# Mixers' branch gates and branch outputs computed token-major

## The chip, the cores and the metric

The kernel runs on one core of a Trainium2 chip. The metric is the device time of one execution in microseconds (us), shown as the median of several. TensorE is called PE here, VectorE DVE, ScalarE ACT, GpSimd POOL, and SyncE SP; SP issues the loads of the weights.

## The reference

Four blocks work on x, 256 tokens of 1024 features, in float32. Two of them (the layers) hold a feed-forward part, a mixer, and another feed-forward part; two more have other mixers and are not touched. A layer's mixer makes three branches of 512 features each from the normed h, gates them and projects the sum:

```
h      = rms_norm(x, mix_norm)
gl     = h @ w_in[:, last 3*1024]                  # three gates of 1024 features
y[0]   = mla_branch(...);  y[1] = gdn_branch(...);  y[2] = moba_branch(...)    # 256 x 512 each
merged = sum over n of  sigmoid(gl[n]) * (y[n] @ w_branch[n])                    # 256 x 1024
x      = x + merged @ w_out
```

The kernel takes tanh(gl / 2) and uses (tanh + 1) as the gate; the factor one half is applied where x is updated.

## The kernel before

**Units.** All weights come as one stream of units, 128 partitions of 1024 float32 numbers (512 KB). SP loads unit u into one of three raw buffers (`raw`, `load`, L492) as soon as the low half of unit u-3 is made. ACT rounds it to `w_hi` (`split`, L550, 128 x 1024), DVE makes `w_lo` = raw - `w_hi` (`split`, L1211). There are six slots; `split(u)` waits until unit u-6 is used (`unit_used`), and its place in the queues of ACT and DVE is written out by hand: `split(u + AHEAD)` with AHEAD = 5 stands where unit u is due on PE. Activations have halves too, `a_hi` and `a_lo`. A product takes three matmuls: high by high, high by low, low by high.

**Gates.** `gate_unit(l, i)` (L2342) makes 128 gate features of all 256 tokens with `fm` (L2196): for each of 8 pieces of K three matmuls with the weights stationary and 256 tokens moving, into the first half of bank 6 or 7 by turns. `gate_tile` (L679) on ACT takes the tanh of the bank, 128 x 256. There are 24 such units a layer. They are spread over the mixer to fill the time in which PE would wait for other engines: units 0 to 3 in the doubling steps that invert a triangular matrix (L2501 to L2528), 4 to 8 behind them, 9 to 17 in the first attention loop (`FILLS`, `LAST_FILL`, L211), 18 to 21 around the second attention's head, the rest in its loop.

**Branches.** `branch_unit(l, i)` (L2349), 12 a layer, makes 256 features of one branch output (two groups of 128, K = 4 x 128), 24 matmuls with 256 tokens moving, into bank 6 or 7 by turns. `merge` (L1446) on DVE multiplies the 512 columns with tanh + 1 and, from the second branch on, adds them to `msum`. Units 0 to 7 fill the second attention loop, units 8 to 11 follow it. ACT and DVE then make the high and low half of `msum`, which is feature-major (`mix_high` L907, and L1812), for the output product `km_tokens` (L2260), where the activations are stationary and 512 columns of the weights move: 12 matmuls a unit, 8 units, banks 0 to 3.

**Attention loop.** Each of its four steps has on PE: a fill, the next scores, the turn of the probabilities, a fill, probabilities by values. DVE takes the maxima (L1421 to L1429), ACT the exponentials (L691, L693), DVE normalises (L1437 to L1439), ACT copies the turned ones (L699). Ahead of the second loop PE turns queries and keys (L2604), which waits for the copies of the query product by ACT (L870 to L876) and for DVE (L1789 to L1797). POOL computes powers (L1131) and masks for the doubling steps (L1146).

Every engine works its own queue in order; a wait at its head holds all that follows.

## Time and profile before

| | |
|---|---|
| median of 3 runs | 1955.2 us (1954.77 to 1956.87) |
| profiled execution | 1960.22 us, span 1958.4 us |
| busy: PE, its weight loads, DVE, ACT, POOL | 99%, 89%, 75%, 56%, 5% |
| DMA from HBM | 327.91 MB, 168 GB/s over the span |
| first mixer, second mixer | from 197 to 497 us, from 869 to 1169 us |

A row of a timeline has the start and the length in us, the engine, the line of the kernel, the operation, what it writes and reads with sizes, and the count of instructions that were merged in it; idle time of the engine before it stands in brackets with what ended it. Matmuls overlap, so the pace of a stream is read from the starts, not from the lengths. All matmuls with an operand that was rounded to halves carry one line, L2155.

### The profile page before, as it was taken

Reading aid. Unit: us, or ns where it says so; the run is one execution under the profiler, and the core shown is the slowest. Engines: PE = TensorE matmul, PEld = TensorE weight load, DVE = VectorE, ACT = ScalarE, POOL = GpSimd, SP = SyncE. Lnnn points to the kernel's source line nnn. Section 1 sums busy time; section 2 is a strip of 40 time slices with the busy share of each in tenths; the row PEclk is TensorE's granted clock in tenths of the full one; section 3 lists DMA queues with packets and bytes.
Section 4 is the critical chain, followed back from the end, with each engine's and each line's share of the span. In section 5 each row is a group of like instructions: output and inputs, shape, how many; then the busy total and the mean of one; then the engine's idle time right before and its main releaser. Section 6 shows DMA issues by size and latency. Waiting matters only on the chain.

```text
span 1958.4 us, 35076 instructions
## 1 busy us (share of the span) xinstructions
PE 1930.7 (99%) x13137; PEld 1734.8 (89%) x13137; DVE 1469.8 (75%) x2252; ACT 1087.9 (56%) x1702; POOL 89.3 (5%) x61
## 2 busy tenths in 40 slices
PE   9999999999999999999999999999999999989999
PEld 8888899999888888889899998889898889879998
DVE  6777777667777777778667777777578888877887
ACT  6555764665555555556536644555345555765554
POOL 0000002010000000000120102000000000100000
PEclk9999999999999999999999999999999999999999
DMA  6656443344555655555424455655655665444554
GB/s 231 194 190 197 160 157 101 114 154 144 168 188 190 193 173 192 193 183 178 132 80 142 140 166 165 199 188 190 203 179 163 195 190 179 158 126 141 193 191 140
DMA packets 95798, 331.03 MB, mean 169 GB/s; under 512 B 10960, under 2 KB 16720, under 8 KB 95568
## 3 DMA queue, kind: packets, MB, share of 16 engines
q1 hardware_dynamic: 93712, 325.91, 51.6%
q10 hardware_dynamic: 1984, 3.68, 0.5%
q8 instruction: 74, 1.21, 0.2%
q14 instruction: 28, 0.23, 0.0%
HBM read 327.91 MB, written 1.64 MB: 168 GB/s over the span
## 4 chain that ended last, share of the span: by engine, by line
PE 82%; DVE 8%; issue 4%; ACT 2%; DMA 2%; POOL 1%; POOLq 0%; SPq 0%; DVEq 0%; ACTq 0%
PE ps L2155 80%; DVE w_lo L1216 3%; DMA raw<-stream 1%; DVE arena L1580 1%; ACT w_hi L557 1%; POOL sc L1131 1%; PE ps L2184 1%; PE ps L2390 1%; PE ps L2604 0%; POOL tmp L1146 0%; DMA x<-x_in 0%; DVE tmp L1306 0%; DVE sc L1690 0%; DVE x L1227 0%; DVE arena L1591 0%
## 5 line engine op out<-in xcount | busy, mean ns | idle before, releaser
L2155 PE MATMUL ps<-a_both,w_hi 128*128 128x256 f32 (+1 forms) x4864 | 993.4, 325 | 3.1 <-DVE w_lo L1216 1.7
L1216 DVE TENSOR_TENSOR w_lo<-raw,w_hi 128x1024 fp32r<-128x1024 f32 x614 | 748.5, 1225 | 247.4 <-ACT w_hi L557 246.8
L2155 PEld LDWEIGHTS ps<-a_both,w_hi 128*128 128x128 f32 x4864 | 814.1, 190 | 80.6 <-DVE w_lo L1216 4.0
L557 ACT ACTIVATE w_hi<-raw 128x1024 fp32r<-128x1024 f32 x614 | 637.5, 1053 | 161.5 <-DMA raw<-stream 97.2
L2155 PE MATMUL ps<-a_both,w_lo 128*128 128x256 f32 x3344 | 661.7, 283 | 0.0
L2155 PEld LDWEIGHTS ps<-a_both,w_lo 128*128 128x128 f32 x3344 | 524.9, 191 | 8.9
L2155 PE MATMUL ps<-w_hi,a_both 128*128 128x512 f32 (+2 forms) x1616 | 505.4, 383 | 2.2 <-DVE w_lo L1216 1.8
L2155 PEld LDWEIGHTS ps<-w_hi,a_both 128*128 128x128 f32 x1616 | 301.3, 189 | 59.8 <-DVE w_lo L1216 2.7
L2155 PE MATMUL ps<-w_lo,a_both 128*128 128x512 f32 (+2 forms) x808 | 308.8, 382 | 0.0
L2155 PEld LDWEIGHTS ps<-w_lo,a_both 128*128 128x128 f32 x808 | 152.7, 189 | 24.3
L1131 POOL TENSOR_TENSOR sc<-sc,nhalf 128x2 f32<-128x2 f32 (+5 forms) x25 | 60.5, 2421 | 1637.6 <-DVE sc L1255 1195.3
L626 ACT ACTIVATE a_both<-arena 128x256 fp32r<-128x256 f32 x132 | 55.3, 419 | 140.1 <-DVE arena L1326 100.9
L615 ACT ACTIVATE arena<-arena 128x256 f32<-128x256 f32 x88 | 36.7, 417 | 159.8 <-DVE arena L1318 144.0
L1285 DVE TENSOR_TENSOR arena<-ps,arena 128x512 f32<-128x512 f32 x114 | 78.7, 690 | 39.8 <-ACT arena L620 38.4
L620 ACT ACTIVATE arena<-ps 128x512 f32<-128x512 f32 x114 | 67.9, 596 | 66.8 <-PE ps L2155 66.6
L1318 DVE TENSOR_TENSOR arena<-arena 128x512 f32<-128x512 f32 x114 | 78.0, 685 | 0.0
L918 ACT ACTIVATE arena<-arena,par 128x256 f32<-128x256 f32 x44 | 26.4, 601 | 88.2 <-DVE arena L1318 78.4
L1331 DVE TENSOR_TENSOR a_both<-arena,a_both 128x256 fp32r<-128x256 f32 x132 | 56.4, 427 | 7.2 <-ACT a_both L626 7.2
L2155 PE MATMUL ps<-arena 128*128 128x128 f32 (+4 forms) x400 | 46.2, 329 | 4.6 <-DVE arena L1723 1.7
L1823 DVE SCALAR_TENSOR_TENSOR arena<-arena,par 128x255 f32<-128x255 f32 x44 | 21.3, 484 | 37.6 <-ACT arena L918 37.5
L2155 PEld LDWEIGHTS ps<-arena 128*64 128x64 f32 (+2 forms) x400 | 33.7, 174 | 12.8 <-DVE arena L1723 2.0
L682 ACT ACTIVATE gates<-ps 128x256 f32<-128x256 f32 x48 | 18.5, 385 | 41.2 <-PE ps L2155 40.8
(333 smaller groups left out, 1257.7 us busy)
## 6 DMA issues: line engine op xcount, KB each, us to landing
raw<-stream SPq DMA_DIRECT2D x613, 512.0 KB, 3.5
arena<-upad SPq DMA_DIRECT2D x8, 284.0 KB, 5.9
gates<-late ACTq DMA_DIRECT2D x1, 1088.0 KB, 5.7
out<-tmp SPq DMA_DIRECT2D x8, 128.0 KB, 2.1
upad<-arena ACTq DMA_DIRECT2D x2, 288.0 KB, 8.0
con<-consts SPq DMA_DIRECT2D x1, 560.0 KB, 5.2
raw<-stream ACTq DMA_DIRECT2D x1, 512.0 KB, 4.2
x<-x_in SPq DMA_DIRECT2D x2, 256.0 KB, 5.2
```

Of the source, the lines that this page charges most:

```text
L557: nc.scalar.activation(w_hi[:, u % SLOTS, :], raw[:, u % RAW, :], ACT.Copy).then_inc(hi_ready, 1)
L615: nc.scalar.activation(th2[:, p, :], gus[:, p, 0:TOK], ACT.Tanh, scale=0.5).then_inc(gate_act, 1)
L620: nc.scalar.activation(glo, ps[:, 4 + 2 * p:6 + 2 * p, TOK:512], ACT.Copy).then_inc(lo_copied, 1)
L626: nc.scalar.activation(a_hi[:, 8 + p, :], gu2[:, p, :], ACT.Copy).then_inc(gu_hi_ready, 1)
L918: nc.scalar.activation(gh2[:, p, :], gus[:, p, 0:TOK], ACT.Identity, scale=w, bias=b).then_inc(conv_in, 1)
L1131: return nc.gpsimd.tensor_tensor(o, i, nhalf[:, 0:n], ALU.pow)
L1216: V.tensor_tensor(w_lo[:, u % SLOTS, :], raw[:, u % RAW, :], w_hi[:, u % SLOTS, :], ALU.subtract).then_inc(split_ready, 1)
L1285: V.tensor_tensor(gus[:, p, :].rearrange("p (a b) -> p a b", b=TOK), ps[:, 4 + 2 * p:6 + 2 * p, 0:TOK], glo, ALU.add).then_inc(gu_added, 1)
L1318: V.tensor_tensor(v, v, each(rrow, 2), ALU.mult).then_inc(gs_ready, 1)
L1331: V.tensor_tensor(a_lo[:, 8 + p, :], gu2[:, p, :], a_hi[:, 8 + p, :], ALU.subtract).then_inc(gu_split, 1)
L1823: V.scalar_tensor_tensor(gh2[:, p, 1:], gus[:, p, 0:TOK - 1], w[1], gh2[:, p, 1:], ALU.mult, ALU.add).then_inc(loop_chain2, 1)
L2155: return nc.tensor.matmul(o, a, b, start=start, stop=stop, **k)
```

## The change

Gates and branch outputs become token-major: the activations are stationary (128 tokens), 512 columns of the weights move, and the result has tokens on partitions. The DRAM stream stays as it is; the loads of gate and branch units gather other pieces of it. Four gate units now form a tile of 512 features (bank 6 for the first 128 tokens, bank 7 for the others), each unit holding a quarter of K; two branch units form a tile of 512 features. The evacuations and merges work on 512 columns of one tile and one half of the tokens; a new semaphore, `tile_done`, tells that the first half of a tile is through, one matmul group ahead of the unit's end. The merged sum is token-major too, so PE turns it in two groups of 8 transposes (`mix_turn`) into banks 4 and 5, then 6 and 7, and the halves for the output product are made from these banks. Branch units 0 and 1 move ahead into the first attention loop, gate units 16 and 17 behind it.

```diff
+        first = [AT["branch", l] + 3 * i + 1 for i in range(4)]
+        take(("branch_first", l), first[:2])
         take(("up", l), [AT["up", l] + 2, AT["up", l], AT["up", l] + 1])
...
-EARLY_GATES = 18
+EARLY_GATES = 16
...
-         ((("g", 15),), (("g", 16),)))
-FILLS = (FILLS, (((("g", 22), ("g", 23)), (("b", 0),)),) + tuple(((("b", 2 * j - 1),), (("b", 2 * j),)) for j in range(1, 4)))
-LAST_FILL = (("g", 17), ("b", 7))
+         ((("g", 15),), (("b", 0),)))
+FILLS = (FILLS, (((("g", 20), ("g", 21)), (("g", 22),)), ((("g", 23),), (("b", 2),)))
+         + tuple(((("b", 2 * j - 1),), (("b", 2 * j),)) for j in range(2, 4)))
+LAST_FILL = (("b", 1), ("b", 7))
...
+        def gate_rows(l, i):
+            lo = AT[("gates_a", "gates_b", "gates_c")[i // 8], l] + 4 * (i // 4 % 2)
+            return stream[lo:lo + 4].rearrange("i p n -> p i n")[:, :, 256 * (i % 4):256 * (i % 4) + 256]
+        def branch_rows(l, i):
+            n, h, kp = (1, 2, 0)[i // 4], i // 2 % 2, i % 2
+            rows = stream[AT["branch", l]:AT["branch", l] + 12].rearrange("(d n) p c -> n p d c", n=3)
+            return rows[n][:, 2 * h:2 * h + 2, 512 * kp:512 * kp + 512]
...
+                if u in relaid:
+                    n, rows = relaid[u]
+                    sp.dma_start(raw[:, u % RAW, :].rearrange("p (i n) -> p i n", i=n), rows).then_inc(raw_loaded[u % RAW], 16)
...
+            def gate_half(l, i, tt):
+                if tt == 0:
+                    act.wait_ge(tile_done, 12 * l + tiles_before(i) + 1)
+                else:
+                    act.wait_ge(unit_used, gate_at(l, i) + 1)
+                nc.scalar.activation(gate_tokens(i // 8, tt, i // 4 % 2), bank(6 + tt), ACT.Tanh, scale=0.5).then_inc(gate_evac, 1)
             def gate_tile(l, i):
-                act.wait_ge(unit_used, gate_at(l, i) + 1)
-                nc.scalar.activation(gates[:, i, :], bank(6 + i % 2, 0, TOK), ACT.Tanh, scale=0.5).then_inc(gate_evac, 1)
+                if i % 4 == 3:
+                    for tt in range(TT):
+                        gate_half(l, i, tt)
...
+                        gate_half(l, EARLY_GATES + 3, 0)
                         exp_scores(8 * l + 4, None, sc[:, 192:208])
-                        late_gate(3)
+                        gate_half(l, EARLY_GATES + 3, 1)
...
+            def mix_high(l, h):
+                act.wait_ge(*PE.at(l, f"mixT{h}"))
+                for q in range(2):
+                    c = 4 * h + 2 * q
+                    nc.scalar.activation(a_hi[:, c:c + 2, :], bank(4 + 2 * h + q).rearrange("p (a b) -> p a b", b=TOK), ACT.Copy).then_inc(mix_hi, 1)
...
+            def merge(l, p):
+                n, h = (1, 2, 0)[p // 2], p % 2
+                for tt in range(TT):
+                    if tt == 0:
+                        dve.wait_ge(tile_done, 12 * l + (7 + p if p else 5))
+                    else:
+                        dve.wait_ge(unit_used, branch_at(l, 2 * p + 1) + 1)
...
+                    m = msum[:, tt, 512 * h:512 * h + 512]
+                    V.scalar_tensor_tensor(mB[:, tt, :] if p > 1 else m, gate_tokens(n, tt, h), 1.0, bank(6 + tt), ALU.add, ALU.mult
+                                           ).then_inc(merge_read, 1)
+                if p > 1:
+                    for tt in range(TT):
+                        m = msum[:, tt, 512 * h:512 * h + 512]
+                        dve.wait_ge(merge_read, 12 * l + 2 * p + tt + 1)
+                        V.tensor_tensor(m, m, mB[:, tt, :], ALU.add).then_inc(mix_ready, 1)
...
+                    if kind and j > 1:
+                        merge(l, j - 1)
...
                 split(fill_at(l, LAST_FILL[kind]) + AHEAD)
-                if kind:
-                    merge(l, 7)
+                merge(l, 3 * kind)
...
+                split(mla + AHEAD)
+                split(mla + 1 + AHEAD)
+                merge(l, 4)
+                split(mla + 2 + AHEAD)
+                mix_low(0)
+                split(mla + 3 + AHEAD)
+                merge(l, 5)
...
             def gate_unit(l, i):
-                fm(gate_at(l, i), bank(6 + i % 2, 0, TOK))
+                for tt in range(TT):
+                    if q == 0:
+                        if p == 0:
+                            pe.wait_ge(zs_ready, 2 * l + tt + 1)
+                        elif i == EARLY_GATES:
+                            pe.wait_ge(merge_read, 12 * l + 2)
+                            if tt:
+                                pe.wait_ge(*AC.at(l, "qcopy"))
+                        else:
+                            pe.wait_ge(gate_evac, 12 * l + 2 * p + tt - 1)
+                    tokens_of(lambda k: a_hi[:, 2 * q + k, 128 * tt:128 * tt + 128], lambda k: a_lo[:, 2 * q + k, 128 * tt:128 * tt + 128],
+                              w_h, w_l, tt, 4, q == 0, q == 3)
+            def tokens_of(hi, lo, w_h, w_l, tt, n, first, last):
+                o = bank(6 + tt).rearrange("p (i o) -> p i o", i=n)
+                for k in range(2):
+                    mm(o, hi(k), w_h[:, k], start=first and k == 0, stop=False)
+                    mm(o, hi(k), w_l[:, k], start=False, stop=False)
+                    e = mm(o, lo(k), w_h[:, k], start=False, stop=last and k == 1)
...
+            def mix_turn(l, h):
+                pe.wait_ge(mix_ready, 8 * l + 2 * h + 6)
+                for c in range(4 * h, 4 * h + 4):
+                    for tt in range(TT):
+                        b = 4 + c // 2
+                        e = nc.tensor.transpose(bank(b, (c % 2) * TOK + 128 * tt, (c % 2) * TOK + 128 * tt + 128),
+                                                msum[:, tt, 128 * c:128 * c + 128], ident)
...
-                for dp in range(4):
-                    branch_unit(l, 8 + dp)
+                for i in range(8, 11):
+                    branch_unit(l, i)
+                mix_turn(l, 0)
+                branch_unit(l, 11)
                 for k in range(KC):
+                    if k == 2:
+                        mix_turn(l, 1)
                     pe.wait_ge(mix_split, 4 * l + k // 2 + 1)
                     km_tokens(POS["out", l] + k, k, k == 0, k == KC - 1)
```

## Rows read from the trace of the kernel before

**Rows 1.** The page: engines, chain, and four of the costliest groups (busy, mean ns).

```profile
PE 1930.7 (99%) x13137; PEld 1734.8 (89%) x13137; DVE 1469.8 (75%) x2252; ACT 1087.9 (56%) x1702; POOL 89.3 (5%) x61
...
PE 82%; DVE 8%; issue 4%; ACT 2%; DMA 2%; POOL 1%; POOLq 0%; SPq 0%; DVEq 0%; ACTq 0%
...
L1216 DVE TENSOR_TENSOR w_lo<-raw,w_hi 128x1024 fp32r<-128x1024 f32 x614 | 748.5, 1225 | 247.4 <-ACT w_hi L557 246.8
...
L557 ACT ACTIVATE w_hi<-raw 128x1024 fp32r<-128x1024 f32 x614 | 637.5, 1053 | 161.5 <-DMA raw<-stream 97.2
...
L620 ACT ACTIVATE arena<-ps 128x512 f32<-128x512 f32 x114 | 67.9, 596 | 66.8 <-PE ps L2155 66.6
...
L682 ACT ACTIVATE gates<-ps 128x256 f32<-128x256 f32 x48 | 18.5, 385 | 41.2 <-PE ps L2155 40.8
```

**Rows 2.** Windows: busy PE, PEld, DVE, ACT, POOL; granted clock, DMA share, GB/s.

```profile
365.00:400.00 35.00, 35.00 (x295) 31.81 (x294) 26.77 (x51) 24.06 (x57) 0.00 (x0) 1.00 0.42 136
...
432.00:475.20 43.20, 43.08 (x355) 40.76 (x354) 34.80 (x55) 23.57 (x46) 0.00 (x0) 1.00 0.41 137
```

**Rows 3.** The gate evacuations: all of them, and the first layer's last seven.

```profile
L682 ACT ACTIVATE gates<-ps x48: 373/383/398, 318.6 to 1102.2; 128x256 f32<-128x256 f32 x48
...
L682 ACT ACTIVATE gates<-ps x7: 373/383/384, 400.9 to 430.0; 128x256 f32<-128x256 f32 x7
```

**Rows 4.** Timeline of PE, branch units: first group, and the output product's first matmul.

```profile
461.12 0.40 PE L2155 MATMUL ps<-a_both,w_hi 128*128 128x256 f32 x2
...
475.16 0.40 PE L2155 MATMUL ps<-w_hi,a_both 128*128 128x512 f32 x1
```

**Rows 5.** Timeline of PE, output product: two starts, 28 groups apart.

```profile
477.00 0.62 PE L2155 MATMUL ps<-w_hi,a_both 128*128 128x512 f32 x2
...
496.04 0.62 PE L2155 MATMUL ps<-w_hi,a_both 128*128 128x512 f32 x2
```

**Rows 6.** Timeline of PE, 8 transposes and the matmuls of a gate unit behind them.

```profile
356.73 1.03 PE L2545 MATMUL ps<-con,arena 128*128 128x128 f32 x8
357.51 0.48 PE L2155 MATMUL ps<-a_both,w_hi 128*128 128x256 f32 x2
357.84 0.28 PE L2155 MATMUL ps<-a_both,w_lo 128*128 128x256 f32 x1
```

**Rows 7.** Timelines of PE (fourth doubling step) and DVE (before the turned keys).

```profile
320.81 1.15 PE L2155 MATMUL ps<-arena,tmp 64*64 64x64 f32 x32 [0.27 <-POOL tmp L1146]
...
414.51 0.68 DVE L1797 TENSOR_TENSOR arena<-arena,sc 128x512 f32<-128x512 f32 x1
```

**Rows 8.** Timelines of ACT and PE ahead of the second attention loop.

```profile
419.51 1.05 ACT L557 ACTIVATE w_hi<-raw 128x1024 fp32r<-128x1024 f32 x1
423.93 0.46 ACT L691 ACTIVATE arena<-ps,sc 128x128 f32<-128x128 f32 x1 [3.37 <-DVE sc L1429]
...
425.90 0.38 ACT L682 ACTIVATE gates<-ps 128x256 f32<-128x256 f32 x1
...
423.21 1.03 PE L2604 MATMUL ps<-con,arena 128*96 128x128 f32 x8
```

**Rows 9.** Timelines of PE (unit 7's start), ACT and DVE around branch unit 7.

```profile
460.66 0.50 PE L2155 MATMUL ps<-a_both,w_hi 128*128 128x256 f32 x2
...
460.95 1.05 ACT L557 ACTIVATE w_hi<-raw 128x1024 fp32r<-128x1024 f32 x1
...
464.37 0.68 DVE L1452 SCALAR_TENSOR_TENSOR arena<-gates,ps 128x512 f32<-128x512 f32 x1
465.09 0.69 DVE L1456 TENSOR_TENSOR arena<-arena 128x512 f32<-128x512 f32 x1
```

**Rows 10.** The raw loads on the page, and the four loads in pieces of 1 KB.

```profile
raw<-stream SPq DMA_DIRECT2D x613, 512.0 KB, 3.5
...
L497 SPq DMA_DIRECT2D raw<-stream x4: 368/371/379, 1711.7 to 1720.3; - x4
...
DMA to landing us min/median/max: 3.5/4.0/4.6
```

More of the change, by code:

```diff
@@ L125, in order @@
         take(("gates", l), gates[:EARLY_GATES])
+        first = [AT["branch", l] + 3 * i + 1 for i in range(4)]
+        take(("branch_first", l), first[:2])
         take(("up", l), [AT["up", l] + 2, AT["up", l], AT["up", l] + 1])
         take(("late_gates", l), gates[EARLY_GATES:])
-        for n, name in ((1, "branch_gdn"), (2, "branch_moba"), (0, "branch_mla")):
+        take(("branch_gdn", l), first[2:])
+        for n, name in ((2, "branch_moba"), (0, "branch_mla")):
             take((name, l), [AT["branch", l] + 3 * dp + n for dp in range(4)])
@@ L491, in _ @@
             sp.dma_start(raw[:, 2, :], stream[2]).then_inc(raw_loaded[2], 16)
+            relaid = {}
+            for l in range(DEPTH):
+                for i in range(24):
+                    relaid[gate_at(l, i)] = 4, gate_rows(l, i)
+                for i in range(12):
+                    relaid[branch_at(l, i)] = 2, branch_rows(l, i)
             def load(u):
@@ L900, in mixer @@
                     split(POS["branch_mla", l] + dp + AHEAD)
-                    if dp:
-                        mix_high(l, dp - 1)
-                mix_high(l, 3)
-                for k in range(KC):
+                mix_high(l, 0)
+                for k in range(3):
                     split(POS["out", l] + k + AHEAD)
-            def mix_high(l, dp):
-                act.wait_ge(mix_ready, 4 * l + dp + 1)
-                nc.scalar.activation(a_hi[:, 2 * dp:2 * dp + 2, :], msum[:, dp, :].rearrange("p (a b) -> p a b", b=TOK), ACT.Copy).then_inc(mix_hi, 1)
+                mix_high(l, 1)
+                for k in range(3, KC):
+                    split(POS["out", l] + k + AHEAD)
+            def mix_high(l, h):
[3 more added lines that the diff above has]
+                    nc.scalar.activation(a_hi[:, c:c + 2, :], bank(4 + 2 * h + q).rearrange("p (a b) -> p a b", b=TOK), ACT.Copy).then_inc(mix_hi, 1)
             def current_tap(F, p, j=0):
@@ L1485, in attention @@
                         rope_tables(l, j)
-                    if kind and j:
-                        merge(l, 2 * j - 1)
                     if j:
@@ L1806, in mixer, with mix_low @@
                 attention(l, 1, 8, None, sc[:, 192:208])
-                for dp in range(4):
-                    split(POS["branch_mla", l] + dp + AHEAD)
-                    merge(l, 8 + dp)
-                    dve.wait_ge(mix_hi, 4 * l + dp + 1)
-                    V.tensor_tensor(a_lo[:, 2 * dp:2 * dp + 2, :], msum[:, dp, :].rearrange("p (a b) -> p a b", b=TOK), a_hi[:, 2 * dp:2 * dp + 2, :],
-                                    ALU.subtract).then_inc(mix_split, 1)
-                for k in range(KC - 1):
+                def mix_low(h):
+                    for q in range(2):
+                        c = 4 * h + 2 * q
+                        dve.wait_ge(mix_hi, 4 * l + 2 * h + q + 1)
+                        V.tensor_tensor(a_lo[:, c:c + 2, :], bank(4 + 2 * h + q).rearrange("p (a b) -> p a b", b=TOK), a_hi[:, c:c + 2, :],
+                                        ALU.subtract).then_inc(mix_split, 1)
+                mla = POS["branch_mla", l]
+                split(mla + AHEAD)
[6 more added lines that the diff above has]
+                for k in range(2):
+                    split(POS["out", l] + k + AHEAD)
+                mix_low(1)
+                for k in range(2, KC - 1):
                     split(POS["out", l] + k + AHEAD)
@@ L2342, in gate_unit @@
             def gate_unit(l, i):
[L2343 to L2365 removed]
+                u, p, q = gate_at(l, i), i // 4, i % 4
@@ new lines, in tokens_of @@
+            def tokens_of(hi, lo, w_h, w_l, tt, n, first, last):
+                o = bank(6 + tt).rearrange("p (i o) -> p i o", i=n)
+                for k in range(2):
+                    mm(o, hi(k), w_h[:, k], start=first and k == 0, stop=False)
+                    mm(o, hi(k), w_l[:, k], start=False, stop=False)
+                    e = mm(o, lo(k), w_h[:, k], start=False, stop=last and k == 1)
+                if tt:
+                    e.then_inc(unit_used, 1)
+                elif last:
+                    e.then_inc(tile_done, 1)
@@ L2620, in mixer @@
                 pe.wait_ge(o_split, 8 * l + 8)
-                for dp in range(4):
-                    branch_unit(l, 8 + dp)
+                for i in range(8, 11):
+                    branch_unit(l, i)
+                mix_turn(l, 0)
+                branch_unit(l, 11)
                 for k in range(KC):
+                    if k == 2:
+                        mix_turn(l, 1)
                     pe.wait_ge(mix_split, 4 * l + k // 2 + 1)
```

69 lines of the change are left out of this document (30 added, 39 removed).

## Prediction

> **What bounds the kernel now.** I read the page's first part, then the chain that ended last, the windows of the first mixer, and last the timeline of each engine there. TensorE is busy for 99% of the span and makes 82% of the chain, VectorE is busy for 75% of it and ScalarE for 56% [rows 1]. In the mixer, from its attention loops to the output product, the PE column fills its windows, 35.00 of 35.00 us and 43.08 of 43.20, at a granted clock of 1.00, so at 2.4 GHz [rows 2]. So what counts in this stage is what PE streams and at what pace, and then each place where PE would have to wait. The two layers run alike: the last gate evacuation of the first starts at 430.0 us, of the second at 1102.2, 672 us later, and there are 48 in all [rows 3]. So I work out one layer and double it.
>
> **Gates and branches: the pace of the matmuls.** A gate unit is now 24 matmuls of 256 columns, a branch unit too. From 461.12 to 475.16 us PE starts 39 groups of three, so a group is 0.36 us, a matmul 0.12 and a unit 2.88 [rows 4]. After the change a unit is 12 matmuls of 512 columns with the activations stationary, which is what the output product does already: 28 groups of three from 477.00 to 496.04 us are 0.68 us each, a matmul 0.227 and a unit 2.72 [rows 5]. The columns streamed are the same; half of the per-matmul cost goes, 0.0133 us for each 512 columns. A layer has 24 gate and 12 branch units, 72 units in all: 72 x 0.16 = **11.5 us less**. One thing is not in any row: the new moving operand is read as four runs of 128 (gates) or two runs of 256 columns (branches) instead of one run of 512. Its pace is bounded by 0.227 us as in [rows 5] and by two 256-column matmuls, 0.24 us, at which the 11.5 us would be 0. I take the first, because operand, type, stationary and output are otherwise those of [rows 5].
>
> The Trainium skill (TensorE: Matmul & The Clock Gate, Back-to-back issue gap) gives a gap of N / 2.4 + 2.5 ns for a warm stream. By that, two 256-column matmuls would cost only 2.5 ns more than one of 512, and the 864 new matmuls would save an estimated 2.2 us in place of 11.5. The trace does not agree: its 0.12 us is over the 0.109 us that the rule gives.
>
> **The turn.** The gated sum is now token-major and the output product needs features on partitions: two groups of 8 transposes a layer. The same shape stands at 356.73 us: 8 transposes take until 357.51, and the matmul behind them comes 0.33 us instead of 0.24 later, together 0.87 us [rows 6]. Four groups: **3.5 us more**, all on PE.
>
> **ScalarE and VectorE.** 24 evacuations of 256 columns (0.38 us) become 12 of 512 (0.60 us, as L620 has them), 9.2 to 7.2 us a layer [rows 1]; the merges are 12 products and 8 sums of 512 columns as before; the high and low halves read PSUM in place of SBUF at the same width. All lies beside PE. Nothing of it counts but where it holds a bank. The turned halves have cover: the first turn stands behind unit 10 (2.72 us), while the last product and the two sums that it needs take 0.68 + 0.69 + 0.69 us [rows 9]; the high and low half behind it take 0.6 + 0.7 us under unit 11. Without that cover each of the two would cost up to 2 us.
>
> **The DMAs.** A gate unit is loaded as 4 pieces of 1 KB for each partition, a branch unit as 2 of 2 KB, instead of 4 KB. Four units of the last mixer are already loaded so: 4.0 us to landing (4.6 at most) against 3.5 [rows 10]. With three raw buffers a load, its high half (1.05 us) and its low half (1.22 us) [rows 1] have three units' time, 8.2 us; 4.6 + 2.3 = 6.9 fits. The queue's order is otherwise kept, so I cost this at nothing; if a landing took over 5.9 us, each further microsecond would cost a third of itself a unit.
>
> **New waits, per layer.** Before, two banks took turns by unit: a bank was free one whole unit (2.88 us) before it was needed. Now both banks belong to one tile of 4 gate or 2 branch units, and the first unit of the next tile needs bank 6 at once and bank 7 half a unit, 1.36 us, later. Most tile ends have other PE work behind them. I find five places where time is lost:
> - The fourth doubling step waits for GpSimd, which lets PE go at 320.81 [rows 7]: the 0.16 us of the gate unit before it is lost.
> - The turn of the keys waits for VectorE's L1797, which ends at 415.19 [rows 7] and hangs on ScalarE's copies of the query product, not on the two gate units before it: 0.31 us lost.
> - Gate 20 opens a tile. Bank 7 comes free by the second evacuation of gate 19, which stands on ScalarE's queue behind the exponentials. These start at 423.93 after the scores' maxima, and their end is the start of L682 at 425.90; the maxima stand behind a low half whose high half starts at 419.51 after a gate evacuation that now falls away [rows 8]. I put them 0.5 us earlier: exponentials to 425.4, evacuation to 426.0. PE turns the last keys at 423.21 [rows 8], now 0.3 earlier, so it starts gate 20 at 423.8 and wants bank 7 at 425.15: 0.85 us. Behind it on PE is everything.
> - Branch unit 8 opens a tile right behind unit 7. VectorE must first take unit 7's low half (its high half runs from 460.95 for 1.05 us, so until 463.2), then product 0 of 0.68 us: 463.9, while PE, which began unit 7 at 460.66, is through at 463.5 [rows 9]: 0.45 us.
> - Unit 10 opens the last tile: the high half for a slot that unit 8 frees starts only at its end, 1.05 + 1.22 us later VectorE is free, and 0.68 more for the product makes 2.95 + 0.2 us against unit 9's 2.72: 0.4 us.
>
> Sum 2.2 us a layer, **4.3 us more**. From both sides: 0 if VectorE and ScalarE reach these places early enough, 3 us a layer if the two branch places and gate 20 each cost half a unit more or so.
>
> **The sum**: -11.5 + 3.5 + 4.3 = -3.7 us. The profiled execution took 1960.2 us with a span of 1958.4; it is 5 us above the median of the three runs, 1955.2, and I carry the difference over as it is: 1951.5 us, -0.19%.
>
> **Rivals.**
> - *The waits do not come*: -11.5 + 3.5 = -8.0, 1947.2 us. For it: VectorE has idle time in every one of these windows [rows 2], and ScalarE's gate evacuations that fall away let its high halves start earlier. Against: the order of the queues is fixed, and the three places above are worked out with it. Chance 0.18.
> - *The operand in pieces streams no faster than two narrow matmuls* (slower than before): each of the 864 matmuls takes 0.24 us, so 0 + 3.5 + 4.3 less the 1.0 us that two of the five waits then do not have: +6.8, 1962 us. It decides from 0.231 us a matmul on, where 864 times the saving is the 7.8 us of turn and waits. Against it: the columns are still whole runs of 512 bytes a partition. Chance 0.12. The skill's gap rule cited above would end on this side too: with its 2.2 us in place of 11.5 the estimate is +5.6, about 1961 us; the pace of [rows 4] speaks against it, so it has little of this chance.
> - *More places wait*: VectorE works 34.80 of 43.20 us in the second attention and the branches [rows 2]; its merges are now taken in blocks of two products and two sums, 2.7 us on one queue, so that a low half or a probability block comes late, and PE stands another 1.5 to 3 us a layer. That gives -1 to +2, about 1955.7 us. Chance 0.17, of it 0.04 slower.
> - *The pieces make DMAs late*: landings over 5.9 us while 48 gate units are fetched; a microsecond over costs 16 us, so it would be seen at once, 1960 us or more. [Rows 10] speak against it. Chance 0.04.
>
> **How the numbers follow.** The forecast case, -1.5 to -6 us, has 0.49. What a measurement of this kernel can tell from no change is about 0.2%, 3.9 us, and -3.7 lies at that edge, so the case is split: 0.26 faster, 0.23 not told apart. Faster: 0.26 + 0.18 = 0.44. Same: 0.23 + 0.13 = 0.36. Slower: 0.12 + 0.04 + 0.04 = 0.20. The forecast case's own range is 1949 to 1954. To hold 8 in 10 the range reaches from the case without waits, 1947, up over the case of more waits to 1958; the rest of the two slow rivals, 0.16, and a little below 1947 stay out.
>
> **What would show it.** Right: groups of 512-column matmuls on a_both and w at 0.68 us for three in the gates; PE idle before matmuls of gate 20 with ScalarE's gate evacuation as releaser, and before branch units 8 and 10 with VectorE's product; two groups of 8 transposes of 0.87 us a layer; mixers shorter by 1.9 us each and the feed-forward stages as before. Wrong: a pace of 0.24 us; waits of ScalarE's high half for the raw loads in the gates; waits of PE at the turns or at output units 0 and 4, whose cover I trust; or a spread of VectorE waits over the second attention.

## The result, and the profile after

The change made the kernel slower by 0.19%, not faster. Its first program took 1961.3 us (median of 15 runs) against 1958.2 for the kernel before (15 runs): ratio 1.0019, 95% interval 1.0011 to 1.0027. Two more programs of the same kernel gave 1.0024 (1.0013 to 1.0034) and 1.0015 (1.0006 to 1.0024). The prediction said 1951.5 us and -0.19%; the measured time lies above its range as well. Of the 9.8 us between 1951.5 and 1961.3, 3.0 are the starting point, 1955.2 us in three runs against 1958.2 in fifteen; what the change itself was to do, -3.7 us, came out as +3.7, and this document is about that difference of 7.4 us.

The profiled execution of the kernel after took 1961.3 us with a span of 1959.5. Its page answers [rows 1]:

```profile
PE 1926.5 (98%) x12305; PEld 1686.6 (86%) x12305; DVE 1469.3 (75%) x2252; ACT 1085.0 (55%) x1678; POOL 89.3 (5%) x61
...
PE 81%; DVE 7%; issue 5%; ACT 3%; DMA 2%; POOL 1%; POOLq 0%; SPq 0%; DVEq 0%; ACTq 0%
...
raw<-stream SPq DMA_DIRECT2D x613, 512.0 KB, 3.7
```

TensorE runs 832 instructions fewer (72 units with 12 matmuls less, 32 transposes more) and is busy 4.2 us less, and the span is no shorter: what left the busy time came back as waits. The windows of the first mixer show where; they are those of [rows 2], moved with the stages, and have the same columns.

```profile
363.00:398.00 35.00, 35.00 (x194) 26.15 (x193) 27.61 (x52) 23.90 (x54) 0.00 (x0) 1.00 0.42 136
430.00:473.50 43.50, 42.66 (x217) 33.15 (x216) 33.20 (x52) 24.13 (x48) 0.00 (x0) 1.00 0.46 144
```

The first attention is full as before; in the second, with the branches, PE now has holes: 0.84 us in 43.5, against 0.12 in 43.2. The waits of PE in the first layer from 288 to 497 us (line that waited, releaser's line, us in total, times, longest):

```profile
PE ps L2220 <- DVE arena L1777: 0.8, 1, 0.8
PE ps L2220 <- DVE arena L1511: 0.8, 2, 0.4
PE ps L2220 <- ACT gates L724: 0.8, 1, 0.8
PE ps L2220 <- DVE arena L1771: 0.6, 3, 0.2
PE ps L2220 <- DVE gates L1805: 0.5, 1, 0.5
PE ps L2220 <- ACT gates L873: 0.4, 1, 0.4
PE ps L2220 <- POOL tmp L1199: 0.4, 1, 0.4
PE ps L2220 <- ACT gates L858: 0.2, 1, 0.2
PE ps L2699 <- DVE arena L1851: 0.2, 1, 0.2
```

Four rows are new or longer than in the kernel before, whose row of GpSimd is this:

```profile
PE ps L2155 <- POOL tmp L1146: 0.3, 1, 0.3
```

Of the four, L724 is the gate evacuation, L1511 the merge's product (twice), L1851 what the turn of the keys waits for, and POOL's went from 0.3 to 0.4. The other five are the same to 0.1 us in both kernels. The timelines of PE put them in their places:

```profile
422.18 0.40 PE L2220 MATMUL ps<-w_hi,a_both 128*128 128x512 f32 x1
423.39 0.50 PE L2220 MATMUL ps<-w_hi,a_both 128*128 128x512 f32 x1 [0.81 <-ACT gates L724]
423.72 0.39 PE L2220 MATMUL ps<-w_lo,a_both 128*128 128x512 f32 x1
...
460.17 0.39 PE L2220 MATMUL ps<-w_hi,a_both 128*128 128x512 f32 x1
460.96 0.47 PE L2220 MATMUL ps<-w_hi,a_both 128*128 128x512 f32 x1 [0.40 <-DVE arena L1511]
...
466.29 0.39 PE L2220 MATMUL ps<-w_hi,a_both 128*128 128x512 f32 x1
467.12 0.47 PE L2220 MATMUL ps<-w_hi,a_both 128*128 128x512 f32 x1 [0.44 <-DVE arena L1511]
...
469.96 1.04 PE L2443 MATMUL ps<-con,arena 128*128 128x128 f32 x8
470.75 0.47 PE L2220 MATMUL ps<-w_hi,a_both 128*128 128x512 f32 x1
...
479.04 1.03 PE L2443 MATMUL ps<-con,arena 128*128 128x128 f32 x8
479.83 0.47 PE L2220 MATMUL ps<-w_hi,a_both 128*128 128x512 f32 x1
```

These are the second half of gate 20, the first halves of branch units 8 and 10, each at the bank that the prediction named, and the two turns, behind which PE goes on at once. Each wait costs more than its bracket: from 422.18 the next matmul should stand 0.23 us on, and it stands 1.21 on, so 0.98; at the two merges 0.56 and 0.60.

**The gate part.** To compare kernels I cut each layer at its first group of transposes ahead of the doubling steps and at the first transpose of the feed-forward block behind it. Between them lie all changed units. Before, then after, first layer:

```profile
289.41 1.03 PE L2480 MATMUL ps<-con,gates 128*128 128x128 f32 x8
...
496.95 0.60 PE L2184 MATMUL ps<-con,x 128*128 128x128 f32 x4
```
```profile
288.41 1.04 PE L2575 MATMUL ps<-con,gates 128*128 128x128 f32 x8
...
496.29 1.28 PE L2249 MATMUL ps<-con,x 128*128 128x128 f32 x9
```

207.54 us before, 207.88 after. This length repeats to 0.1 us between the two layers and between programs of one kernel, so it can be read to that. There is one exception, the second layer of e2_pieces with 210.93 us: two instructions of VectorE took 2.2 us longer than elsewhere (1.52 and 2.31 us in place of 0.42 and 1.22), PE waited 2.2 us for L1730 in place of 0.2, and a stretch at a lower clock followed, of which more below. The two gate parts together are 0.6 us longer (415.67 us against 415.07; in the copies 415.71 each against 415.09 and 415.10); the prediction had 3.7 us shorter. That is 4.3 us of the miss, and the experiments take it apart. The rest of the measured +3.7 us lies outside the gate parts, in code that is the same in both kernels; it has the last group of experiments.

### The profile page after: what moved, and what is told of

The parts are those of the page before. It is cut to its first block, busy times and chain, and to the rows that moved or that the text cites. A ratio compares the mean times of both kernels' runs of the same rounds, so it can differ in the third digit from the quotient of the medians.

```text
span 1959.5 us, 33368 instructions
## 1 busy us (share of the span) xinstructions
PE 1926.5 (98%) x12305; PEld 1686.6 (86%) x12305; DVE 1469.3 (75%) x2252; ACT 1085.0 (55%) x1678; POOL 89.3 (5%) x61
## 4 chain that ended last, share of the span: by engine, by line
PE 81%; DVE 7%; issue 5%; ACT 3%; DMA 2%; POOL 1%; POOLq 0%; SPq 0%; DVEq 0%; ACTq 0%
PE ps L2220 79%; DVE w_lo L1269 2%; DMA raw<-stream 2%; ACT w_hi L596 2%; POOL sc L1184 1%; PE ps L2485 1%; PE ps L2249 1%; DVE arena L1634 0%; DMA x<-x_in 0%; POOL tmp L1199 0%; DVE tmp L1359 0%; DVE sc L1744 0%; DVE x L1280 0%; DVE arena L2050 0%; DVE a_both L1356 0%
## 5 line engine op out<-in xcount | busy, mean ns | idle before, releaser
L1269 DVE TENSOR_TENSOR w_lo<-raw,w_hi 128x1024 fp32r<-128x1024 f32 x614 | 748.7, 1225 | 246.7 <-ACT w_hi L596 246.1
L2220 PE MATMUL ps<-a_both,w_hi 128*128 128x512 f32 (+1 forms) x3712 | 778.5, 336 | 2.4 <-DVE w_lo L1269 1.7
L2220 PE MATMUL ps<-w_hi,a_both 128*128 128x512 f32 (+2 forms) x2192 | 701.1, 388 | 5.8 <-DVE w_lo L1269 1.8
L2220 PEld LDWEIGHTS ps<-a_both,w_hi 128*128 128x128 f32 x3712 | 635.3, 190 | 75.5 <-DVE w_lo L1269 3.1
L2220 PE MATMUL ps<-a_both,w_lo 128*128 128x256 f32 x2768 | 499.0, 283 | 0.0
L2220 PEld LDWEIGHTS ps<-w_hi,a_both 128*128 128x128 f32 x2192 | 409.1, 188 | 92.3 <-issue 6.0
L2220 PEld LDWEIGHTS ps<-a_both,w_lo 128*128 128x128 f32 x2768 | 414.8, 191 | 8.9
L2220 PE MATMUL ps<-w_lo,a_both 128*128 128x512 f32 (+2 forms) x1096 | 421.9, 385 | 0.0
L2220 PEld LDWEIGHTS ps<-w_lo,a_both 128*128 128x128 f32 x1096 | 206.8, 189 | 33.6
L1379 DVE SCALAR_TENSOR_TENSOR arena<-arena 128x256 f32<-128x256 f32 x88 | 39.0, 444 | 3.0
```

The source lines that it names most:

```text
L1269: V.tensor_tensor(w_lo[:, u % SLOTS, :], raw[:, u % RAW, :], w_hi[:, u % SLOTS, :], ALU.subtract).then_inc(split_ready, 1)
L1379: V.scalar_tensor_tensor(gu2[:, p, :], a2[:, p, :], 0.25, gus[:, p, TOK:512], ALU.mult, ALU.mult).then_inc(gu_ready, 1)
L2220: return nc.tensor.matmul(o, a, b, start=start, stop=stop, **k)
```

## Experiments

Gate part of the first layer, and what was timed (a dash: one profiled execution only):

```
kernel      gate part us   vs before   ratio to before (95%)
before      207.54
after       207.88         +0.34       1.0019 (1.0011 to 1.0027)
e1_host     207.89         +0.35       1.0021 (1.0012 to 1.0030)
e2_pieces   207.54          0.00       0.9996 (0.9985 to 1.0006)
e5_pace     204.03         -3.51       0.9974 (0.9964 to 0.9984)
e8_noturn   206.38         -1.16       -
e6_gate20   206.72         -0.82       -
e7_merges   206.48         -1.06       -
e3_order    205.41         -2.13       0.9989 (0.9979 to 0.9998)
e4_both     205.40         -2.14       0.9986 (0.9975 to 0.9997)
n4_order    205.36         -2.18       0.9987 (0.9978 to 0.9996)
```

**e1_host: the same matmuls on an operand in one run.** The kernel after, with the host's packing changed so that gates and branch weights arrive token-major:

```diff
-            fm(AT["gates_" + "abc"[i], l], gl[:, 1024 * i:1024 * i + 1024])
+            for h in range(2):
+                tm(AT["gates_" + "abc"[i], l] + 4 * h, gl[:, 1024 * i + 512 * h:1024 * i + 512 * h + 512])
...
-                o = bank(6 + tt).rearrange("p (i o) -> p i o", i=n)
+                o = bank(6 + tt)
```

> The changed kernel with the host laying gate and branch weights out token-major, so that a unit is one run of 4 KB a partition in DRAM and a run of 512 columns as moving operand; nothing else differs. Theory A (the cost is on TensorE: turns, waits at tile ends, and the first groups of 512-column matmuls after a switch being slower): no change against the changed kernel, so about +0.2% against the kernel before, and the same three places of waiting. Theory B (loads in pieces cost the 3 us that the two profiles do not show): 3 us less than the changed kernel, so within 0.05% of the kernel before. Theory C (the operand in runs of 128 columns streams slower): the groups of three in the gates fall from 0.70 to 0.68 us at once, 1.5 us a layer less.

The gate part is the same to 0.01 us and the time too. Neither the strided moving operand nor the loads in pieces are what the change lost.

**e2_pieces: the loads alone.** The kernel before, with its gate and branch units loaded in 1 and 2 KB pieces:

```diff
+                if u in relaid:
+                    n, rows = relaid[u]
+                    sp.dma_start(raw[:, u % RAW, :].rearrange("p (i n) -> p i n", i=n), rows).then_inc(raw_loaded[u % RAW], 16)
```

> The kernel before with only the loads of gate and branch units in pieces of 1 and 2 KB (its weights are then other ones, so gates and branch outputs are not the reference's; the work is the same). Theory A: within 0.05% of the kernel before, as every load still has cover. Theory B: +3 us, +0.15%, with ScalarE's high halves waiting longer for loads in the mixers.

No change in the first layer's gate part, 0.9996 in the time. The 72 loads in pieces take longer to land, a median of 3.5 us and 5.4 at most against 3.3 and 4.6 for the same units of the kernel before; in the kernel after it is 3.6 and 5.8. That is still below the 5.9 us from which the prediction would have had a price, and PE waits no longer for it. The rival of late DMAs falls, and the zero that the prediction put there stands.

**e5_pace: the form of the matmul alone.** The kernel before, unit for unit in its own order and banks, with each gate and branch unit as 12 matmuls of 512 columns:

```diff
-                fm(gate_at(l, i), bank(6 + i % 2, 0, TOK))
+                tokens12(u, bank(6 + i % 2), 2 * (i % 4))
...
+            def tokens12(u, o, c):
+                for tt in range(TT):
+                    tk = slice(128 * tt, 128 * tt + 128)
+                    for k in range(2):
+                        w = slice(512 * k, 512 * k + 512)
+                        mm(o, a_hi[:, c + k, tk], w_hi[:, s, w], start=(tt == 0 and k == 0), stop=False)
+                        mm(o, a_hi[:, c + k, tk], w_lo[:, s, w], start=False, stop=False)
+                        q = mm(o, a_lo[:, c + k, tk], w_hi[:, s, w], start=False, stop=(tt == 1 and k == 1))
```

> The kernel before with only the form of the matmuls exchanged: each gate and branch unit is 12 matmuls of 512 columns with the activations stationary, into one bank, instead of 24 of 256; banks, waits, evacuations, merges and loads are those of before, there is no turn (its gates and branch outputs are sums of other pieces than the reference's). It gives the term of the pace alone. Theory as predicted (0.16 us a unit wherever it stands): 36 x 0.16 less 0.47 us behind the two waits on other engines = 5.3 us a layer from the first turn of the decay blocks to the mixer's end (207.5 us in the kernel before), 10.6 us in all, 0.5% below the kernel before. Theory A (after a switch of form the first three groups take 0.70 us instead of 0.68, so a unit between other work saves only 0.10 us): about 3.6 us a layer, 7.2 us in all, 0.37% below.

-3.51 us a layer. PE's view of waits in this gate part has some new ones: 0.3 at the turn of the keys, 0.2 at a merge, 0.1 more at POOL. Without these the form gives 4.1 us for 36 units, 0.114 us a unit, where the prediction had 0.16. Read unit by unit, from its first matmul to the next instruction, it is 4.2 us: the 7 units that follow another unit save 0.15 us on average, the 29 that start behind other work 0.11. The timelines show why. First a gate unit between attention products in the kernel before, then the same place in the kernel after:

```profile
373.57 0.50 PE L2155 MATMUL ps<-a_both,w_hi 128*128 128x256 f32 x2
373.91 0.28 PE L2155 MATMUL ps<-a_both,w_lo 128*128 128x256 f32 x1
374.02 0.40 PE L2155 MATMUL ps<-a_both,w_hi 128*128 128x256 f32 x2
...
376.62 0.93 PE L2155 MATMUL ps<-arena 64*128 64x128 f32 x8
```
```profile
371.44 0.50 PE L2220 MATMUL ps<-w_hi,a_both 128*128 128x512 f32 x1
371.78 0.40 PE L2220 MATMUL ps<-w_lo,a_both 128*128 128x512 f32 x1
372.02 0.63 PE L2220 MATMUL ps<-w_hi,a_both 128*128 128x512 f32 x2
...
372.72 0.62 PE L2220 MATMUL ps<-w_hi,a_both 128*128 128x512 f32 x2
...
373.41 0.62 PE L2220 MATMUL ps<-w_hi,a_both 128*128 128x512 f32 x2
...
374.42 0.93 PE L2220 MATMUL ps<-arena 64*128 64x128 f32 x8
```

A unit that stands alone takes 3.05 us before (2.88 in the stream) and 2.98 after (2.72 in the stream). Both forms lose about 0.1 us on their first instructions; the wide form then runs its first groups at 0.70, 0.70 and 0.69 us and not at 0.68, which eats the rest: this unit saves 0.07 us, and the one ahead of it, 369.72 to 372.76 against 367.71 to 370.64, saves 0.11. The same slow first groups stand in e1_host, where the operand is one run, so they belong to the fresh start and not to the stride.

**e8_noturn: one transpose in place of eight in each turn.** The kernel after, with 14 of 16 transposes a layer left away:

```diff
-                for c in range(4 * h, 4 * h + 4):
-                    for tt in range(TT):
+                for c in (4 * h,):
+                    for tt in (0,):
```

> The changed kernel with 1 transpose instead of 8 in each of the two groups a layer (the output product then works on wrong sums). If the turn lies on the path with its full time, 7 x 0.098 us a group less, 1.4 us a layer: 84.6 us in the same stretch. Rival: ScalarE and VectorE do not have the halves ready, TensorE waits before output unit 0 or 4, and less is gained.

206.38 against 207.88: 14 transposes cost 1.50 us, 0.107 each, so a group of 8 is 0.86 and the two 1.7 us a layer. The timeline above has 0.79 us from the start of a turn to the next matmul and 0.32 in place of 0.23 behind it, together 0.88. The term of 3.5 us stands to 0.1.

**e6_gate20, e7_merges, e3_order: what stands ahead in the queues.** If the waits come because an evacuation or a product is queued behind other work, an exchange in the queue removes them. The first edit moves gate 19's second half ahead of the exponentials, the others the merges ahead of a split that PE doesn't need yet:

```diff
                         gate_half(l, EARLY_GATES + 3, 0)
-                        exp_scores(8 * l + 4, None, sc[:, 192:208])
                         gate_half(l, EARLY_GATES + 3, 1)
+                        exp_scores(8 * l + 4, None, sc[:, 192:208])
...
-                split(fill_at(l, LAST_FILL[kind]) + AHEAD)
+                if kind == 0:
+                    split(fill_at(l, LAST_FILL[kind]) + AHEAD)
                 merge(l, 3 * kind)
+                if kind:
+                    split(fill_at(l, LAST_FILL[kind]) + AHEAD)
...
-                split(mla + 1 + AHEAD)
                 merge(l, 4)
+                split(mla + 1 + AHEAD)
```

e6_gate20 has the first, e7_merges the other two, e3_order all three, and e4_both adds e1_host's packing.

> The changed kernel with three places in two queues exchanged: ScalarE evacuates gate 19's second half before the exponentials, VectorE takes the merges of branch tiles 3 and 4 before the low half that stood in front of each. Theory A: the waits at gate 20 (0.85 us) and at branch units 8 and 10 (0.7 us each with the restart) go, 2.2 us a layer, 4.4 us in all: about 0.05% below the kernel before. Rival: the exponentials come 0.5 us later and the low halves 2 us later, and TensorE waits there instead, so less than half of the 4.4 us is seen.

> Both edits together, the host's layout and the three exchanges. Theory A: as with the exchanges alone, 4.4 us below the changed kernel. Theory B: 7 us below it, 0.2% below the kernel before. Theory C: as B, with the gain in the gates' pace.

> The changed kernel with only ScalarE's exchange (both halves of gate 19 evacuated before the exponentials). Read from the first turned queries to the mixer's end, 85.96 us in the changed kernel and 83.43 with all three exchanges: this one's share should be 0.8 to 0.9 us, 85.1 us. Rival: the exponentials it delays take back half of it.

> The changed kernel with only VectorE's exchanges (merges of branch tiles 3 and 4 before the low half ahead of each). In the same stretch its share should be the two waits with their restarts, 0.69 + 0.73 us, and what the faster start leaves: 84.5 us, where the three exchanges together give 83.43.

Gate 20 gives back 1.16 us a layer, the merges 1.40, all three 2.47: within 0.1 of the sum. e4_both has the gate part of e3_order to 0.01 us, so the host's packing adds nothing here either. In e3_order's waits over the same stretch as above, the rows of the gate evacuation and of the merges are gone; the rest is as it was:

```profile
PE ps L2223 <- DVE arena L1780: 0.8, 1, 0.8
PE ps L2223 <- DVE arena L1774: 0.6, 3, 0.2
PE ps L2223 <- DVE gates L1808: 0.5, 1, 0.5
PE ps L2223 <- ACT gates L873: 0.4, 1, 0.4
PE ps L2223 <- POOL tmp L1199: 0.4, 1, 0.4
PE ps L2223 <- ACT gates L858: 0.2, 1, 0.2
PE ps L2702 <- DVE arena L1854: 0.2, 1, 0.2
```

The three waits cost 2.5 us a layer, not the 1.7 that the prediction gave these three. VectorE's timeline in the kernel after shows the order at both merge places, low half (L1269) first, and then the two products in a block:

```profile
458.99 1.23 DVE L1269 TENSOR_TENSOR w_lo<-raw,w_hi 128x1024 fp32r<-128x1024 f32 x1 [0.52 <-ACT w_hi L596]
460.13 1.28 DVE L1511 SCALAR_TENSOR_TENSOR arena<-gates,ps 128x512 f32<-128x512 f32 x2
...
465.15 1.23 DVE L1269 TENSOR_TENSOR w_lo<-raw,w_hi 128x1024 fp32r<-128x1024 f32 x1 [1.40 <-ACT w_hi L596]
466.29 1.28 DVE L1511 SCALAR_TENSOR_TENSOR arena<-gates,ps 128x512 f32<-128x512 f32 x2
```

VectorE stands idle for 1.40 us ahead of the second low half, but the merge could not have filled that time: unit 9 runs from 463.80 us, and the first half of it, which the merge reads, streams for 1.36 us, until about where the low half starts. What the exchange takes out of the way is the low half. The product starts 2.5 us into unit 9 here and 1.6 us into it in e7_merges, where unit 9 begins at 463.52:

```profile
465.08 0.69 DVE L1511 SCALAR_TENSOR_TENSOR arena<-gates,ps 128x512 f32<-128x512 f32 x1
```

With the exchanges the kernel beats both: 1953.8 us, ratio 0.9989 (0.9979 to 0.9998), and again 0.9987 (0.9978 to 0.9996) as a second program.

**The 3 us outside the gate parts.** Copies of the kernels, as programs of their own, ask whether the medians are to be trusted.

> The kernel before, unchanged, as a second program. What is asked: the medians put the kernel after at +0.19% (+3.7 us), while its two gate parts together are only 0.7 us longer in the traces; 3 us are open. Theory A (the rest is real and lies in the stretches in front of the gate parts and elsewhere): this program gives a ratio of 1.000 with an interval of about +-0.001, and what its profile shows outside the two gate parts (its span less 2 x 207.5) lies near 1540 to 1541, as in the look with loads in pieces (1539.6), 2 us below the profile of before (1543.3). Theory B (the rest is the spread of one program against another): the ratio lies off 1.000 by 0.001 or more, or its remainder lies anywhere between 1539 and 1546.

> The kernel before once more, for a further profile. Gate parts 207.5 us each in either theory. Theory A: the remainder outside them 1540 to 1541, and no wait over 0.8 us for the sums of squares of the keys (L844) in layer 1's mixer before its gate part. Theory B: anywhere between 1539 and 1546, with such a wait in some profiles.

> The kernel after, unchanged, as a second program. Theory A: ratio 1.0019 again, gate parts 207.9 each, a remainder of 1542 to 1545, and in layer 1's mixer before its gate part a wait of 1.0 to 1.2 us for the sums of squares of the keys. Theory B: ratio anywhere from 1.000 to 1.002 (gate parts alone: 0.7 us of 1957 is 1.0004), and a remainder that does not differ from that of the copies of before.

> The kernel after with the three queue exchanges, as a second program. Gate parts 205.4 each in either theory. Theory A: ratio 0.9989 again (its gate parts alone, -4.3 us, would be 0.9978). Theory B: ratio from 0.998 to 0.9995.

The copy of before gave 0.9992 (0.9983 to 1.0001), that of after 1.0024. So one program differs from another of the same kernel by up to about 0.1%, and the kernel after is slower by more than that. Theory A's numbers for the rest did not hold: spans less their two gate parts are 1543.3, 1538.8 and 1543.0 us in three profiles of before and 1543.8, 1540.8 and 1541.3 in three of after. Their means differ by 0.3 us. The wait that theory A named did come, though. In the second layer's mixer, ahead of its gate part, PE waits for ScalarE's squares of the keys before it sums them, first in the kernel before, then in the kernel after:

```profile
940.21 4.15 PE L2155 MATMUL ps<-ones,tmp 128*128 128x1 f32 x32
```
```profile
941.35 4.26 PE L2220 MATMUL ps<-ones,tmp 128*128 128x1 f32 x32 [1.23 <-ACT tmp L844]
```

It is 1.23, 1.19 and 1.23 us in the three profiles of after and at most 0.15 in the three of before; 0.96 to 1.19 in e1_host, e6_gate20, e7_merges and e8_noturn, 0.49 in e2_pieces and 0.77 in e5_pace, 0.34 to 0.77 in the three delayed kernels below, and 0.00 to 0.90 in the three programs with all exchanges. A second place is in the last mixer, where PE waits for VectorE's L2097 (L2032 before): 1.6, 1.8 and 2.1 us against 1.6, 0.3 and 1.1. In all, PE is idle outside the gate parts for 23.5, 22.1 and 22.3 us in after and 21.8, 18.8 and 21.0 in before, 2.1 us more on average. What holds ScalarE and VectorE up there was not taken apart.

In the spans this is hidden by a scatter that has a cause in the traces. In every profile the granted clock falls from 1.00 to 0.50, so from 2.4 to 1.2 GHz, at the same three places outside the gate parts: behind the 128x1 matmuls of the sums of squares in both mixers' first halves, and around a wait of 4.0 us for VectorE in the last mixer. e7_merges has a fourth, at 1707.2 us behind a wait of 1.91 us, and a fall at the very end of the program is not counted here. Windows of the kernel before and of after, in the first mixer (the granted clock is the third number from the end):

```profile
266.00:270.00 4.00, 3.77 (x26) 3.15 (x25) 3.62 (x8) 3.84 (x4) 0.00 (x0) 1.00 0.45 157
272.00:277.00 5.00, 5.00 (x24) 5.00 (x25) 1.70 (x6) 0.90 (x1) 2.90 (x1) 0.50 0.16 60
279.00:283.00 4.00, 4.00 (x19) 3.32 (x18) 0.62 (x1) 1.50 (x3) 0.00 (x0) 1.00 0.74 250
```
```profile
273.00:275.00 2.00, 2.00 (x12) 2.00 (x11) 0.46 (x3) 0.78 (x1) 2.00 (x1) 0.50 0.44 172
```

The same 16 products ("ps<-arena" behind the sums) take 2.91 us in the one and 1.95 in the other:

```profile
275.74 2.91 PE L2155 MATMUL ps<-arena 128*128 128x128 f32 x16
```
```profile
275.72 1.95 PE L2220 MATMUL ps<-arena 128*128 128x128 f32 x16
```

The stretch at 0.50 lasts 3.4 us at some places and 6.8 at others, and each 3.4 us of it lose 1.7 us of full clock; the profiles hold between 3 and 7 such steps. e7_merges has seven and e6_gate20 four, and the first is 5.2 us longer outside the gate parts, 5.1 of them by the three steps. It isn't all of the scatter: n1_before has one step less than before and is 4.5 us shorter, 3 of them by PE's idle time, 18.8 us against 21.8. The Trainium skill (TensorE: Matmul & The Clock Gate, Part 1) describes such a gate with these two levels; the levels agree with the rows.

Every execution, also those without a profile, has its mean granted clock on record, and its time goes with it. For the kernel before, 35 executions at 0.997 took 1956.1 us on average, 51 at 0.996 took 1957.4 and 12 at 0.995 took 1960.0; for the kernel after it is 1959.1 (10), 1960.5 (6) and 1961.8 (11). So at the same clock after is 1.8 to 3.2 us longer. Its clock is also lower, 0.9956 on average of 34 against 0.9962 of 103, which is 1.2 us of full clock.

Does the change add such steps? The last runs make only the gate parts of the kernel before longer, ahead of gate unit 22:

```diff
+                if i == 22:
+                    for _ in range(3):
+                        mm(bank(6, 0, TOK), w_hi[:, u % SLOTS, 0:128], a_hi[:, 0, :], start=True, stop=True)
```

> The kernel before with 3 more matmuls of 256 columns in each layer's gate part, ahead of gate unit 22, that write what the next one overwrites: 3 x 0.12 = 0.36 us a layer, 0.7 us in all, as much as the gate parts of the kernel after are longer. Theory C (the time outside the gate parts hangs on when the stages begin, through how often the granted clock falls to half): the time rises by more or less than the 0.7 us (1.0004) by a step or two of 1.7 us, to about 1.0013 or 1.0021 if it is what happened to the kernel after. Theory D (the excess belongs to the new matmul form or to its loads, not to the moment): 1.0004, within the interval of about +-0.001.

> The same with 8 more matmuls a layer: 0.96 us a layer, 1.9 us in all, 1.0010 by the matmuls alone. Theory C: off that by a step of 1.7 us or more, in a direction that need not be that of the one with 3 (below 1.000 or above 1.0019). Theory D: 1.0010.

> The same with 15 more matmuls a layer: 1.8 us a layer, 3.6 us in all, 1.0018 by the matmuls alone. Theory C: off that by 1.7 us or more (below 1.0009 or above 1.0027). Theory D: 1.0018.

> The kernel after, unchanged, as a third program. Both theories: gate parts 207.9 each and a ratio of 1.0019 to 1.0024 again. Theory C: its profile shows the clock at half outside the gate parts for 4 to 7 stretches of 3.4 us, the longer of them in the last mixer (6.8 us rather than the 3.4 us of the kernel before).

```
kernel      gate parts both, vs before   as a ratio   measured (95%)
s3_delay    +0.7 us                      1.0004       1.0003 (0.9994 to 1.0012)
s8_delay    +1.9                         1.0010       1.0015 (1.0006 to 1.0024)
s15_delay   +3.6                         1.0018       1.0013 (1.0004 to 1.0022)
n5_after    +0.6                         1.0003       1.0015 (1.0006 to 1.0024)
```

Each delayed kernel lies where its added matmuls alone put it, within its interval; no step of 1.7 us is seen for a stage that begins later. Theory C isn't borne out, but a part of a step can't be ruled out: s15_delay's executions have a clock of 0.9969 against 0.9963 in the same session, 1.2 us less lost, and its time lies about 1 us below what the matmuls give. Nor do the profiles of the two kernels bear out more steps: 5, 4 and 5 in three of before, 4 each in three of after, though n5_after and n3_after have the 6.8 us in the last mixer that theory C forecast. In the last mixer alone the kernels with 512-column units have two steps or more in 8 of 11 profiles, and those with the old form in 1 of 7, a mean of 1.8 against 1.1; that would be 1.2 us, but it is a count of few profiles, and for the kernel after itself the first mixers' steps make up for it.

## Why the prediction was wrong, point by point

- **What bounds the kernel**: right. PE is the bound in the gate parts, and every experiment moved them by what it added to or took from PE.
- **The pace (-11.5 us)**: the mechanism was right, the size too large. It measured -8.2 to -8.4 us (2 x 4.1 by e5_pace's length, 2 x 4.2 unit by unit). "72 x 0.16" took the pace in the stream, from [rows 4, 5], for units of which 29 of 36 start behind other work; the wide form is slower there for its first three groups. 3.1 us of the miss. The estimate from the gap rule of the Trainium skill (TensorE: Matmul & The Clock Gate, Back-to-back issue gap), 2.2 us, was further off than the rows were.
- **The turn (+3.5)**: right, 3.4 to 3.5 us by e8_noturn. The cover of the turns held: no wait at either turn or behind.
- **ScalarE and VectorE, the DMAs (0)**: right, by e2_pieces and e1_host. The median landing of all raw loads was 3.7 us in the kernel after's profile, 3.5 and 3.6 in its copies', and 3.5 before; no row of the gate part's waits has a raw load.
- **New waits (+4.3)**: all five came, where they were put. The three at the banks were mis-sized: 1.7 us a layer against 2.5, 1.16 for gate 20 and 1.40 for the two merges. The idle times themselves were forecast well: 0.85, 0.45 and 0.4 against brackets of 0.81, 0.40 and 0.44. What was missing is that a wait costs more than its idle time, 0.98 + 0.56 + 0.60 = 2.1 us to the next matmul, and that the stream behind it starts slowly again: units 8 and 10 take 2.84 us and not 2.72, which makes 0.56 + 0.60 + 0.24 = 1.40 us, as e7_merges has it, and gate 20's unit takes 3.94 us against 2.85 in e6_gate20.
- **The sum**: by the experiments, a layer is -4.2 (pace) + 1.7 (turn) + 2.5 (banks) + about 0.4 (POOL and the keys) = +0.4 us, against +0.34 read in the gate part. The two terms that failed are the pace, 3.1 us, and the waits, about 1.5; less 0.1 at the turn that is 4.5 us for the 4.3 of the miss in the gate parts. The other 3.1 us belong to a term that the sum doesn't have: it took everything outside the gate parts to stay as before.
- **The rivals**: "the waits do not come" fell. "The operand in pieces streams no faster" had the sign of the result and the wrong mechanism: e1_host has no pieces and the same time. "The pieces make DMAs late" fell. "More places wait" was nearest: in the gate parts the waits cost more, but at the named places; outside them two waits that it had not named are longer.
- **What stays open**: the gate parts explain +0.6 us of the measured +3.7 (34 runs of three programs of after have a mean of 1961.1 us, 118 of before 1957.3). About 3 us lie outside. They aren't the loads (e2_pieces) nor the stride (e1_host has them too), and a later start of the stages alone doesn't bring them (s3_delay to s15_delay). On record are two differences that would make up most of them: 2.1 us more idle time of PE, 1.1 of it at the sums of squares of the keys, in three profiles of each, and a mean clock lower by 1.2 us. Neither was taken away by an edit, and the profiled executions themselves have less of the low clock in after, so this is a count and not a proof. Kernels with the wide form and without the waits at the banks show some of the 3 us: e3_order is 4.3 us shorter in its gate parts and 2.2 in the time, e5_pace 7.0 and 5.1. Why the same code waits longer there, and why the clock is lower, is open.

## What to carry to other kernels

Price a wider matmul with the unit where it stands: a pace read in a long stream holds for the stream only, and a short unit between other products gives back a third of the gain. When two banks no longer alternate by unit but both go with a tile, list every tile's first unit and look at what stands ahead of the evacuation in its queue; here three exchanges in the order of two queues turned a slower kernel into one that beats both. And compare the stretch that a change touches, which repeats to 0.1 us, before comparing times that differ by 4 us between runs; then compare the idle time and the granted clock of the rest as well, since equal spans can hide both.

## What the runs showed of the hardware

- A stream of matmuls starts slowly. Behind other products or a wait the first 512-column matmul takes 0.30 to 0.35 us to the next one, and the three groups from there 0.70, 0.70 and 0.69 us against 0.68 in the stream.
- A wait of PE costs more than its idle time: 0.98 us for a bracket of 0.81, 0.56 for 0.40, 0.60 for 0.44.
- Profiles of one kernel differ by up to 4.5 us outside the gate parts, partly through stretches of 3.4 or 6.8 us at the lower clock, behind a burst of 128x1 matmuls and around a 4.0 us wait, partly through idle time of PE (18.8 to 21.8 us in three of before).
- Raw loads of 512 KB in 1 KB and 2 KB pieces landed 0.2 us later than the same units in 4 KB pieces: a median of 3.5 us against 3.3, in e2_pieces and in before.
- A moving operand in four runs of 128 or two of 256 columns streams like one run of 512: the gate part is 207.88 us in after and 207.89 in e1_host.
